# Three buffers for split weight tiles in place of four, and two more places for loaded tiles

## What is computed

```python
def swiglu(h, w_gu, w_down):
    g, u = jnp.split(h @ w_gu, 2, axis=-1)
    return (jax.nn.silu(g) * u) @ w_down

def moe_swiglu(h, w_router, w_gu, w_down):
    logits = (h @ w_router).astype(jnp.float32)
    top_vals, top_idx = lax.top_k(logits, TOP_K)
    top_w = jax.nn.softmax(top_vals, axis=-1)
    combine = jnp.sum(jax.nn.one_hot(top_idx, N_EXPERTS, dtype=jnp.float32) * top_w[..., None], axis=-2)
    out = jnp.zeros_like(h)
    for e in range(N_EXPERTS):
        out = out + combine[..., e:e + 1] * swiglu(h, w_gu[e], w_down[e])
    return out
```

## Time and profile before

| | us |
|---|---|
| median of 3 runs | 1497.15 (1497.05 to 1499.03) |
| profiled execution | 1496.27 |
| its span | 1494.5 |
| PE busy | 1442.2 |
| DVE busy | 993.7 |
| ACT busy | 745.6 |

### The profile page before, as it was taken

One profiled execution on the slowest core, in us unless ns is written; L12 is line 12 of the kernel. 1 busy time (PEld: TensorE's weight loads), 2 busy tenths in 40 slices (PEclk: granted clock), 3 DMA queues, 4 the chain that ended last, 5 costly groups with the idle time before them and its releaser, 6 DMA issues.

```text
span 1494.5 us, 18765 instructions
## 1 busy us (share of the span) xinstructions
PE 1442.2 (97%) x6964; PEld 983.9 (66%) x6964; DVE 993.7 (66%) x1270; ACT 745.6 (50%) x977; POOL 13.8 (1%) x18
## 2 busy tenths in 40 slices
PE   7989999999999999999999999999999989999998
PEld 2836787888789888674666556756565655565573
DVE  2578788888569889764666646765654555655563
ACT  3574544443456885353546445644453444545361
POOL 0000000000000000000100000000000000000000
PEclk9999999999999999999999999999999999999999
DMA  9878698888265335679999999999999999999996
GB/s 363 330 275 283 247 396 309 289 301 295 89 228 171 100 107 208 259 291 407 371 410 404 410 376 416 418 419 421 407 420 413 420 419 413 417 419 415 420 420 255
DMA packets 117018, 501.80 MB, mean 336 GB/s; under 512 B 13635, under 2 KB 16348, under 8 KB 81848
## 3 DMA queue, kind: packets, MB, share of 16 engines
q1 hardware_dynamic: 115640, 496.51, 85.2%
q0 software_dynamic: 1280, 4.01, 0.8%
HBM read 498.33 MB, written 2.29 MB: 335 GB/s over the span
## 4 chain that ended last, share of the span: by engine, by line
PE 81%; DMA 8%; DVE 7%; ACT 3%; issue 1%; SPq 0%; DVEq 0%; ACTq 0%
PE acc L2677 17%; PE acc L2685 17%; PE acc L2678 16%; PE acc L3179 15%; DVE w_lo L1582 3%; DMA raw_rest<-in_moe_w_down 1%; DMA raw<-in_moe_w_down 1%; DMA mod<-in_moe_w_gu 1%; PE xb L3063 1%; DMA raw<-in_moe_w_gu 1%; DMA mod<-in_moe_w_down 1%; ACT w_hi L1038 1%; PE acc L2826 1%; DMA raw<-in_ada_w 1%; PE xb L2725 1%
## 5 line engine op out<-in xcount | busy, mean ns | idle before, releaser
L1582 DVE TENSOR_TENSOR w_lo<-raw,w_hi 128x1024 fp32r<-128x1024 f32 x356 | 427.4, 1221 | 135.6 <-ACT w_hi L1038 125.7
L1038 ACT ACTIVATE w_hi<-raw 128x1024 fp32r<-128x1024 f32 x356 | 370.9, 1057 | 253.7 <-PE acc L2685 151.6
L2677 PE MATMUL acc<-w_hi,g_hi 128*128 128x512 f32 x448 | 179.3, 400 | 4.8 <-ACT w_hi L1038 4.8
L2678 PE MATMUL acc<-w_hi,g_lo 128*128 128x512 f32 x448 | 174.9, 390 | 0.0
L2677 PE MATMUL acc<-w_hi,a_hi 128*128 128x512 f32 x384 | 153.5, 400 | 0.8
L2678 PE MATMUL acc<-w_hi,a_lo 128*128 128x512 f32 x384 | 149.9, 390 | 0.0
L2685 PE MATMUL acc<-w_lo,g_hi 128*128 128x512 f32 x448 | 139.2, 392 | 4.7 <-DVE w_lo L1582 4.6
L3179 PE MATMUL acc<-raw,g_s 128*64 128x512 f32 x592 | 131.7, 595 | 0.7 <-DMA raw<-in_moe_w_gu 0.6
L2685 PE MATMUL acc<-w_lo,a_hi 128*128 128x512 f32 x384 | 118.4, 390 | 0.0
L1582 DVE TENSOR_TENSOR w_lo<-mod,w_hi 128x1024 fp32r<-128x1024 f32 x66 | 78.5, 1220 | 58.3 <-ACT w_hi L1038 56.5
L2677 PEld LDWEIGHTS acc<-w_hi,g_hi 128*128 128x128 f32 x448 | 84.2, 188 | 39.3 <-issue 11.8
(11 more groups left out here) (414 smaller groups left out, 2073.6 us busy)
## 6 DMA issues: line engine op xcount, KB each, us to landing
raw<-in_moe_w_gu SPq DMA_DIRECT2D x136, 1024.0 KB, 15.5
raw<-in_moe_w_down SPq DMA_DIRECT2D x66, 1024.0 KB, 17.3
raw<-in_ada_w SPq DMA_DIRECT2D x96, 512.0 KB, 6.2
mod<-in_moe_w_gu SPq DMA_DIRECT2D x40, 1024.0 KB, 15.5
raw<-in_ffn_w_gu SPq DMA_DIRECT2D x56, 512.0 KB, 6.0
mod<-in_moe_w_down SPq DMA_DIRECT2D x23, 1024.0 KB, 17.4
raw_more<-in_moe_w_gu SPq DMA_DIRECT2D x22, 1024.0 KB, 14.2
raw<-in_ssm_w_in SPq DMA_DIRECT2D x40, 512.0 KB, 4.8
```

The lines of the kernel that those rows point to most:

```text
L1038: act.activation(w_hi[:, w % SPLIT, :], raw_tile(no), ACT.Copy).then_inc(hi_ready, 1)
L1582: dve.tensor_tensor(w_lo[:, w % SPLIT, :], raw_tile(no), r32(w_hi[:, w % SPLIT, :]), ALU.subtract).then_inc(raw_used, 1)
L2677: pe.matmul(o, l_hi[:, k, rows_], hi[:, col:col + HALF], start=new, stop=False)
L2678: pe.matmul(o, l_lo[:, k, rows_], hi[:, col:col + HALF], start=False, stop=False)
```

## The change

`SPLIT` goes from 4 to 3 and `RAW` from 12 to 14: one buffer of `w_hi` and one of `w_lo` become two homes of `raw`. `EARLY["moe"]` follows SPLIT. `FIRST_LOADS` names the two new homes, 12 and 13, and gets one more entry, so that tiles 0 to 31 of the first place are loaded ahead of the router's counts where it was 0 to 29. The low halves that are made early in moe go one by one.

```diff
-RAW = 12
+RAW = 14
 RAW_EXTRA, RAW_ONCE = 8, 10
-SPLIT = 4
+SPLIT = 3
@@
-                   (26, "once4", "once5"), (20, "once6", "once7"), (6, 8, 9), (8, 10, 11), (10, 0, 1), (12, 2, 3),
+                   (26, "once4", "once5"), (20, "once6", "once7"), (6, 8, 9), (8, 10, 11), (10, 12, 13), (12, 0, 1), (30, 2, 3),
                    (22, "mod2", "mod3"), (24, "mod4", "mod5"), (15, "rest8"))
@@
                 if n:
-                    early_lo("moe", n, 2 * n)
+                    early_lo("moe", n, n + 1)
```

## The result

| | before | changed |
|---|---|---|
| median of 4 runs, us | 1497.28 (1497.05 to 1499.03) | 1516.14 (1514.14 to 1517.62) |
| profiled execution, us | 1496.27 | 1516.58 |
| its span, us | 1494.5 | 1514.8 |
| mean granted clock | 0.999 | 0.993 |

The account below looks back on a forecast made before the run. PE was taken to bound the kernel up to the experts, the loads from 890 us on. Ffn gates +10.7, stage starts +3.7 and homes -2.5 gave +11.9 on 1496.27, a median of 1509.0 us; range 1502.9 to 1516.2.

Parts of the forecast that it names:

- rival B: Large experts: PE, ACT and DVE take turns over three buffers, 5 us more, 1514 to 1521; chance 0.13.
- The ffn's gates: Ffn group ends: the split now starts ahead of silu, its low half ahead of the gate's product; +10.7 us.
- the other tiles of the ffn: Ffn tiles away from the gates: low halves still come two tiles ahead of their use; 0 us.
- The starts of stages: Norm1, norm2, dt rows and start of moe: work behind later splits is delayed; together +3.7 us.
- Norm1: First norm: the split of tile 21 waits for tile 18 and delays Square; +0.9 us (0.5 to 1.3).
- Norm2: Second norm: early tile 105's low half makes L1742 start late, half hidden; +0.4 us (0.1 to 0.9).
- Dt rows: Proj: L1411's read stands behind the split of tile 112, which waits for tile 109; +1.5 us (1 to 2).
- Start of moe: Early low halves ahead of the router's sums wait for moe's first tiles, so counts come late; +0.9 us (0 to 2).
- The gain: Experts' loads: two more homes leave two tiles fewer to load behind the last dip; -2.5 us.
- A: Rival: loads swallow the delays and two homes close all dips, gaining 10.6 us; sum -3.3, 1493.9 us; chance 0.05.
- C: Rival: homes bring nothing, each being held longer; +13.3, 1510.4 us; shares the forecast's 0.70.
- D: Rival: homes only take tiles 30 and 31 ahead of the counts, nothing afterwards; time as C, shares the forecast's 0.70.

Follow-up runs that it names:

- changed_again: The changed kernel itself, unaltered, run once more on another chip against the kernel before: 1515.64 us, ratio 1.0113.
- wait3_ahead: The kernel before, four buffers and twelve homes, but ACT waits for tile w - 3 for split tiles ahead of the experts: 1516.58 us, ratio 1.0124.
- wait3_experts: The kernel before, with the wait for tile w - 3 only from the experts' fifth split tile on: 1499.53 us, ratio 1.0009.
- no_pair_30: The changed kernel without the load of tiles 30 and 31 ahead of the router's counts, still 14 homes: 1516.07 us, ratio 1.0114.

## Why the prediction was right

It said +11.9, 1509.0 us, with 1502.9 to 1516.2 as the lowest and highest sum, and it was 1516.14, 18.9 more by the medians. The mechanism was right and so was nearly every place; two terms were mis-sized (tile 64's wait in the ffn, and the homes' gain), and the clock wasn't in it. That the time lies inside the range at all is luck in part: it is 0.1 us below the highest sum, and 2 to 4 us of it are of the clock, for which the range had no term. It lies outside the 1504 to 1514 that had 0.70, in the band of rival B, whose mechanism did not show.

**The ffn's gates**, 10.7 said. Group 1: 2.4 said, 2.41 measured where the clock held. Groups 2 to 6: 1.60 said, 1.66 each. Group 7: 0.3 said, 0.40. This is the step on which all rested, and the four rows of one group gave it to a tenth. Missed was 0.78 at tile 64: there PE turns h (L3063) and waits for a slot that DVE's `mod` (L1637) frees, which stands behind a low half and two sums of `ada` rows:

```profile
296.93 1.23 DVE L1582 TENSOR_TENSOR w_lo<-raw,w_hi 128x1024 fp32r<-128x1024 f32 x1 [1.49 <-ACT w_hi L1038]
298.07 1.41 DVE L1619 SCALAR_TENSOR_TENSOR ada<-raw,cond,ada 128x512 f32<-128x512 f32 x2
299.40 1.28 DVE L1637 TENSOR_TENSOR mod<-xb,mod 128x512 f32<-128x512 f32 x2
...
300.23 1.23 PE L3063 MATMUL xb<-square,h 128*128 128x128 f32 x8 [0.41 <-DVE mod L1637]
```

The low half now starts on ACT's split, after 1.49 us of waiting, and pushes the rest. The term "the other tiles of the ffn" had 0 for this and named a DVE that sums `ada` rows as what would break it; I had not looked at what else is queued behind a low half. Together the stage is 12.0.

**The starts of stages**, 3.7 said. Norm1: 0.9 said, 0.77. Norm2: 0.4, 0.31. Dt rows: 1.5 said, 1.55 at tile 110, by the very wait:

```profile
449.45 0.31 PE L3239 MATMUL xb<-square,dt_rows 32*128 32x32 f32 x2 [1.47 <-ACT dt_rows L1411]
```

which ACT's two rows explain, the split and behind it the read:

```profile
448.07 1.06 ACT L1038 ACTIVATE w_hi<-raw 128x1024 fp32r<-128x1024 f32 x1 [3.57 <-PE acc L2685]
449.04 0.36 ACT L1411 ACTIVATE dt_rows<-xb 32x256 f32<-32x256 f32 x1
```

But proj has 0.38 more at tile 134, and the term was no price of that wait alone: with it gone, others cost as much. Start of moe: 0.9 said. The counts do come 0.9 late: the first load behind them goes out 19.05 us later than before (667.28 against 648.23), the first tile ends 18.18 later. On PE the first tile comes 0.46 earlier against wout's last one, where PE's wait for DVE's `g_lo` is 1.0 us in place of 1.5 (one split fewer stands ahead of the gathered activations on ACT; neither kernel with the wait alone has this gain), and 0.87 is lost at tile 165:

```profile
668.50 0.74 PE L2685 MATMUL acc<-w_lo,g_hi 128*128 128x512 f32 x2 [0.59 <-DVE w_lo L1582]
...
730.54 0.73 PE L2685 MATMUL acc<-w_lo,g_hi 128*128 128x512 f32 x2 [1.57 <-DVE w_lo L1582]
```

The second of these rows is the earlier trace rows again, 1.57 us then and now. Together 3.4. Ahead of tile 260 the waits come to 15.4 us where 14.4 was said.

**The gain**, -2.5 said. At tile 369 it was there: 2.0 to 2.4 us in all seven profiles with 14 homes, and not in the four with 12. At the end it is 0.1 to 0.6 in the profiles without a late fall of the clock, and by the medians some 1 us against the kernels with 12 homes, with intervals that overlap. The step that failed is the one from "two tiles ahead at the last dip" to "two tiles less at the end": I took it that behind 890 only the loads' sum counts, and didn't look at whether a stretch starts on a load of one tile or of two. That accounts for about 1 us of what is given back; the 0.5 to 1.4 us between tile 369 and 453 stay open. The early pair, which I counted as part of the change's merit, gives nothing.

**The clock.** The terms measured come to 15.4 less 0.1 to 0.6 us. By the medians the change costs 18.9, by the ratio 1.0116 17.4; the 2 to 4 us between are not in any wait. They go with the clock: its mean is 0.993 in the profiled run against 0.999 in that of before, and each fall ahead of the experts costs some 1.5 us. On the chip of changed_again the kernel before has 0.993 to 0.998 in eleven runs, 0.9962 in the mean, and the changed kernel 0.994 to 0.995 in four. So, by an estimate from these clocks, the changed kernel has one more of them a run there; on the first chip the other runs of before have no clock on record. In the eleven profiles other than that of before there are 28 falls, all at six places (about 83, 155, 185, 418, 1220 and 1435 us), never at all six. PE's wait of 2.5 us in the first group was followed by one in four of the six profiles that have it, and none of the six in which that wait is shorter or absent has one there. What decides is open: each profile is one execution, and no run counts falls with the waits of one place taken away.

**The rivals.** A (the loads swallow the delays) is refuted by wait3_ahead, and its gain of 10.6 us by the 2.0 to 2.4 measured. B (the large experts bound by the loop, 5 us) is refuted by wait3_experts: the ratio's upper end, 1.0019, is 2.8 us. C (the homes bring nothing) is wrong at tile 369 and nearly right at the end, and its sum (+13.3) was nearer to the truth than the forecast's. D (the homes give only the early pair) is refuted by no_pair_30, which gains 2.0 us from tile 260 to 369 without the pair. One reading of the section on what bounds the kernel was wrong as well: the loads stand still not once but also in the ffn's end (0 GB/s from 400 to 405 us); nothing of the sum hangs on it.

The Trainium skill ("Perfetto Trace Analysis", Optimization Strategy) says that a gap that repeats on the engine that should be saturated can mean too few buffers. The direction agreed: the weight loads' six small gaps of 2.8 us in all became seven of 14.1 when a buffer was taken away. But a buffer is not the only cure: with the gates ahead in the program they are 4.1 us in six with three buffers as well.

## What to carry to other kernels

A ring's depth is also a distance in the program: with S buffers, each instruction written behind the fill of buffer w inherits a wait for item w - S. Taking one buffer away moves every one of these waits a step later, so look for work that stands directly behind a fill and is itself waited for, and put it ahead. With four buffers the gate could stand behind the split at k == 2; with three it had to stand ahead of it. And look at what allows a saturated stretch to start: here the loads waited for the router's counts, and time lost ahead of them was not absorbed (18.1 us at the experts' first tile, 18.2 at tile 369).

## What was unexpected of the hardware

- The granted clock fell for 3.4 us to the lower level in some executions and not in others of the same program, with the same wait ahead (2.48 us: 0.63 us a matmul in one profile, 0.40 in the other). 20 of the 28 falls came at or just behind waits of PE of 1.0 to 2.5 us. The other eight, at about 155 and 418 us, where the norms are, had no wait of more than 0.44 us in the six us before; PE ran narrow matmuls there, as ahead of the fall at 423 us in changed_again:

```profile
420.07 2.05 PE L2737 MATMUL xb<-square,mod 1*128 1x128 f32 x16
```

  The kernel before has the same matmuls and waits of 2.1 us at 1201 and 1208 us, and no fall in its profile. Medians of kernels that differ by less than 2 us are hard to tell apart for that, while the ends of tiles in two profiles can be, up to the first fall.
- ACT's table load costs what its row says and no more: the load at 182.90 in the changed kernel takes 1.28 us and silu starts at 184.19.

```profile
181.82 1.06 ACT L1038 ACTIVATE w_hi<-raw 128x1024 fp32r<-128x1024 f32 x1 [1.66 <-PE acc L2685]
182.90 1.28 ACT L1296 ACT_TABLE_LOAD   x1
184.19 1.08 ACT L1296 ACTIVATE h<-acc 128x512 f32<-128x512 f32 x2
```

The Trainium skill ("ScalarE: Activation LUTs", What ACT_TABLE_LOAD costs) has 1283 ns for the load, which agrees, and another 1380 ns for a drain with each switch of table; by that page, as an estimate, silu would have started near 185.6. The measurement decides: no such time is in this trace.
